# The query projection of a two-block fp32 kernel as three products of rounded parts, and its gate turned later

## The chip, the cores and the metric

The kernel runs on one core of a Trainium2 chip, as one program. The metric is the time of one execution on the device in microseconds (us), lower is better.

## The reference, cut to what matters

Two transformer blocks follow each other, all in fp32. The change lies in the first layer of the second block: its grouped-query attention, over 256 latent tokens and 256 context tokens together (512), with width 1024.

```python
h_lat = x * (1.0 + sc_a) + sh_a
h_ctx = xc * (1.0 + csc_a) + csh_a
...
q, k, v = jnp.split(h @ w_qkv, [16 * 64, (16 + 4) * 64], axis=-1)
q = rms_norm_2(q.reshape(b, n, 16, 64), q_norm)
k = rms_norm_2(k.reshape(b, n, 4, 64), k_norm)
v = v.reshape(b, n, 4, 64)
if rotate:
    q = apply_grid_rope(q, rope)
    k = apply_grid_rope(k, rope)
...
y_lat = block_attention(q_lat, k_all, v_all) @ w_o
y_ctx = block_attention(q_ctx, k_ctx, v_ctx) @ w_o
x = layer_norm(alpha * x + g_a * y_lat, ln_g[i, 0], ln_b[i, 0])
xc = layer_norm(alpha * xc + cg_a * y_ctx, ln_g[i, 0], ln_b[i, 0])
```

Here `x` is what the first block gives, normed by `norm_final`. The context `xc` is an input. The gates `g_a` and `cg_a` are rows of width 1024, one for each stream.

## The kernel before, in words

Every engine has its own program, written out by hand, and semaphores tie them together. A generator per block and engine gives the order; nothing is scheduled by a planner.

- **PSUM.** Eight banks in four pairs: `PROJ`, `SC`, `PT`, `OT`. A `Banks` object knows in which order the fills of a pair follow. `claim` waits until the bank's fill before was taken, `arrived` waits for a fill, `taken` for its release.
- **Weights.** The queue of SyncE (SP) loads tiles of 128 x 4096 numbers (2 MB) into a ring of four slots: `0kv` (keys and values), `0q0`, `0q1` (queries), `0wo0`, `0wo1` (output projection), then the MLP's.
- **Two kinds of matmul.** A plain fp32 `mm` (L2129) leaves two records in the trace. The large ones of the MLPs are done as `product`: each operand is split into a rounded part (`high`, type fp32r) and the rest (`low`), and three fp32r matmuls (L282, L283, L284) replace one plain one. `Split` keeps the weights' parts: GpSimd (POOL) makes `high` by a cast in `round_high` (L263), VectorE (DVE) subtracts and writes `low` over the weight in its slot in `make_low` (L270).
- **The projection, `gqa_project`.** The tokens stand transposed and modulated in `hT` (8 chunks of 128 x 512). PE makes half of the values (`0v1`), and between its two token tiles the transposes of the latent tokens (`xT0`, `xT1`), then ten tiles of 128 rows x 512 tokens, `0a0` to `0a9`: two of keys, eight of queries. Each is eight plain `mm` of 128 x 512. After tile n PE makes the mean square of tile n-1 (`square_mean`) and the rotated halves of tile n-2 (`swap`). ScalarE (ACT) copies and squares tile n, and makes the inverse root for tile n-1 (Ln, then Exp, `scale_of`, L2450 and L2452). DVE multiplies by it (L2671) and rotates (`rotate`, L2659 to L2662). The other half of the values (`0v0`) comes last, and attention waits for the last tiles.
- **The keys' copies.** After each rotated key tile POOL copies it to where attention reads it (L2865, four copies each).
- **The first block's end.** `x_done(t)` is true once DVE has added the last product to token tile t (L1740). ACT then squares the tile (L2557), DVE takes a reciprocal (L2786) and scales the tile by it and by `norm_final` (L2787, a SCALAR_TENSOR_TENSOR whose two wide inputs lie in SBUF). PE's transposes of the latent tiles wait for that.
- **The gate.** `widen` (DVE, L2601) copies a gate's column to all columns, `turn_gate` makes eight transposes on PE (two fills), `take_gate` copies the two fills into `gate_rows` on ACT. For `ga` both streams are turned in the projection, one before `0a0` and one after it.
- **The rest.** Attention over 16 heads, then the output projection (`0wo..`) with residual and layer norm, then the MLP, then the second layer.

In these words T(n) stands for the moment at which ACT begins to copy tile `0a(n)`, which is just after its last matmul.

Of the kernel before, what the change touches and what calls it, by code (L numbers as in the profile page):

```python
# [15 lines left out]
P = 128  # L16
# [44 lines left out]
WORK = 30336  # L61
# [169 lines left out]
class Split:  # L231
# [22 lines left out]
    def high(self, i):  # L254
        _, k, n = self.part(i, True).shape
        return self.buffers[i % len(self.buffers)][:, 0:k * n].rearrange("p (k n) -> p k n", k=k)

    def round_high(self, nc, pool, i):

        self.weights.arrived(pool, self.parts[i][0])  # L260
        if i >= len(self.buffers):
            pool.wait_ge(*self.freed[i - len(self.buffers)])
# [10 lines left out]
    def arrived(self, pe, name, which):  # L273

        i = self.order[name, which]
        pe.wait_ge(self.cut, i + 1)
        return self.high(i), self.part(i, True)

# [41 lines left out]
def first_layer(nc, l, T, dram, out, sem, chip, prev):  # L320
# [204 lines left out]
    for kind, i in step_tiles:  # L525
# [30 lines left out]
    Y = Split(sem, "in", W, chip["ring_low"], chip["ring_high"], parts, freed)  # L556
    halves = [(f"up{i}", b, "n", 2 * P * b, 2 * P) for i in range(8) for b in range(2)]
    halves += [(f"down{i}", b, "k", 2 * b, 2) for i in range(8) for b in range(2)]
    X = Split(sem, "ff", W, chip["ring_low"], early_high + late_high, halves,
              [done(f"up{n}") for n in range(16)] + [(down_used, n + 1) for n in range(15)])  # L560
# [1307 lines left out]
def second_block(nc, T, dram, out, sem, chip, prev):  # L1868
# [8 lines left out]
    hT = work.take(KD, 2 * S)  # L1877
    gate_rows = work.take(2, D)
# [16 lines left out]
    g_v = g.take(4, KV_HEADS * HD)  # L1895
    g_turn = g.take(4, 6, S)
    g_yT = g.take(KD, 2 * S)
    before = Carver(g_turn.rearrange("p a b c -> p (a b c)"))
    g_sq, g_rs, g_rot = before.take(2, 512), before.take(2, 512), before.take(S)
# [56 lines left out]
    for i in range(DEPTH):  # L1956
# [14 lines left out]
        outs += [name for s in range(streams) for name in gate_fills(i, "ga", s)]  # L1971
        outs += [f"{i}o{c}" for c in range(PAIRS)] + [f"{i}wo{t}{h}" for t in range(NT[i]) for h in range(2)]
        score += [name for s in range(streams) for name in gate_fills(i, "gm", s)]
# [16 lines left out]
    GATE = {"ga": OT, "gm": SC}  # L1990
# [62 lines left out]
    X = Split(sem, "mlp", W, chip["ring_low"], half_high, halves, freed)  # L2053
# [7 lines left out]
    nf_scale = sem("nf_scale")  # L2061
    x_first = sem("x_first")
# [25 lines left out]
    cut_base = [0, NT[0] + 2]  # L2088
# [21 lines left out]
    def sync(sp):  # L2110
# [8 lines left out]
        for n, name in enumerate(("ln_g_2", "ln_b_2")):  # L2119
            sp.dma_start(ln_rows[:, n, :], dram[name][0, 0].partition_broadcast(P)).then_inc(first_in, 16)  # L2120
# [6 lines left out]
    def tensor(pe):  # L2127
# [24 lines left out]
        def turn_gate(i, kind, s):  # L2152

            pe.wait_ge(gate_wide, gate_count[i, kind, s])
            for h, name in enumerate(gate_fills(i, kind, s)):
                ps = GATE[kind].claim(pe, name)
# [856 lines left out]
```

## Time and profile before

| what | value |
|---|---|
| median of 3 runs | 2234.24 us (2232.54 to 2234.58) |
| the profiled execution, its own time | 2231.0 us |
| its span, first to last instruction | 2229.2 us |
| mean granted TensorE clock | 0.993 |
| TensorE (PE) busy | 2171.3 us, 97% |
| VectorE, ScalarE, GpSimd busy | 1255.8, 668.7, 484.5 us |

A page of the profile gives busy times by engine. The chain that ended last follows the work back from the last instruction, at each step to what released it. The timeline gives instructions in order of time. Times in all of them count from the start of the span.

### The profile page before, as it was taken

To read this page: it belongs to the slowest core of one execution; us is meant where nothing else is said; L and a number is where in the kernel's file an instruction comes from. 1 tells how busy PE (TensorE), PEld (TensorE's weight loads), DVE (VectorE), ACT (ScalarE), POOL (GpSimd) and SP (SyncE) were. 2 spreads that over 40 slices of the span, in tenths; PEclk is the share of its full clock that TensorE was granted. 3 is DMA by queue.
4 is the path that set the end of the run, shared out by engine and by line. 5 is a ranking of instruction groups with operands and counts; after the bars stand their busy time and mean duration, and the time that the engine had idled before them with its cause. 6 is when DMAs were issued, how large, how long until landed. Compare 5 with 4: busy or idle time off the path is not lost.

```text
span 2229.2 us, 32724 instructions
## 1 busy us (share of the span) xinstructions
PE 2171.3 (97%) x13766; PEld 1768.3 (79%) x13766; DVE 1255.8 (56%) x1678; ACT 668.7 (30%) x1488; POOL 484.5 (22%) x259
## 2 busy tenths in 40 slices
PE   7999999999999999999999999999999999999998
PEld 7998878899889997878898745557888886556887
DVE  5686445865455765449654316665434444457666
ACT  2223453033012234440330267713112023362111
POOL 2222112334322221113433000102111110102332
PEclk9999999999999999999999999999999999999999
DMA  9534667646566346675556503022232314213551
GB/s 267 179 130 141 238 225 225 250 152 227 171 161 224 119 147 225 230 245 200 216 189 218 175 0 120 1 76 95 78 111 78 111 52 106 80 64 123 198 189 57
DMA packets 225959, 339.57 MB, mean 152 GB/s; under 512 B 58988, under 2 KB 94807, under 8 KB 225815
## 3 DMA queue, kind: packets, MB, share of 16 engines
q1 hardware_dynamic: 224720, 333.98, 43.5%
q0 software_dynamic: 944, 3.47, 0.5%
q8 instruction: 110, 1.80, 0.3%
q14 instruction: 35, 0.28, 0.0%
q10 hardware_dynamic: 150, 0.04, 0.0%
HBM read 335.38 MB, written 2.10 MB: 151 GB/s over the span
## 4 chain that ended last, share of the span: by engine, by line
PE 92%; DVE 4%; ACT 2%; issue 1%; SPq 1%; DMA 0%; POOL 0%; DVEq 0%; ACTq 0%
PE bank L282 22%; PE bank L284 21%; PE bank L283 21%; PE bank L2129 15%; PE bank L655 6%; PE bank L2132 2%; PE bank L1000 2%; PE bank L658 1%; SPq L222 1%; DVE ring_low L270 1%; ACT work L1135 1%; ACT L1135 1%; PE bank L952 1%; DVE work L1704 0%; DVE work L1700 0%
## 5 line engine op out<-in xcount | busy, mean ns | idle before, releaser
L283 PE MATMUL bank<-hT_high,ring_low 128*128 128x256 f32 (+1 forms) x2048 | 604.0, 295 | 0.0
L283 PEld LDWEIGHTS bank<-hT_high,ring_low 128*128 128x128 f32 x2048 | 388.8, 190 | 12.2 <-issue 0.7
L263 POOL CAST ring_high<-ring 128x2048 fp32r<-128x2048 f32 (+1 forms) x108 | 204.7, 1895 | 674.8 <-PE bank L284 544.1
L270 DVE TENSOR_TENSOR ring_low<-ring,ring_high 128x2048 fp32r<-128x2048 f32 (+1 forms) x108 | 242.3, 2245 | 123.4 <-POOL ring_high L263 123.2
L282 PE MATMUL bank<-hT_low,ring_high 128*128 128x256 f32 (+1 forms) x1008 | 295.4, 293 | 6.5 <-DVE ring_low L270 4.7
L284 PE MATMUL bank<-hT_high,ring_high 128*128 128x256 f32 (+1 forms) x1008 | 285.0, 283 | 0.0
L263 POOL CAST half_high<-ring 128x2048 fp32r<-128x2048 f32 x64 | 130.5, 2042 | 625.1 <-PE bank L284 452.6
L282 PE MATMUL bank<-ring_low,hidden_high 128*128 128x512 f32 x640 | 251.3, 393 | 0.0
L1135 ACT ACTIVATE work<-bank 128x384 f32<-128x384 f32 (+11 forms) x246 | 109.6, 468 | 386.9 <-PE bank L284 358.3
L270 DVE TENSOR_TENSOR ring_low<-ring,half_high 128x2048 fp32r<-128x2048 f32 x64 | 152.7, 2391 | 95.9 <-POOL half_high L263 95.5
L282 PEld LDWEIGHTS bank<-hT_low,ring_high 128*128 128x128 f32 (+1 forms) x1008 | 192.2, 191 | 15.4 <-issue 8.0
L284 PEld LDWEIGHTS bank<-hT_high,ring_high 128*128 128x128 f32 (+1 forms) x1008 | 190.6, 189 | 0.4
L282 PE MATMUL bank<-hT_low,half_high 128*128 128x256 f32 (+1 forms) x528 | 176.4, 334 | 3.2 <-DVE hT_low L2606 2.5
L284 PE MATMUL bank<-hT_high,half_high 128*128 128x256 f32 (+1 forms) x528 | 176.3, 334 | 0.0
L284 PE MATMUL bank<-half_high,hidden_high 128*128 128x512 f32 x384 | 152.4, 397 | 0.0
L283 PE MATMUL bank<-half_high,hidden_low 128*128 128x512 f32 x384 | 149.8, 390 | 0.0
L2581 ACT ACTIVATE work<-bank 128x512 f32<-128x512 f32 x48 | 28.8, 600 | 375.6 <-PE bank L284 375.6
L282 PEld LDWEIGHTS bank<-ring_low,hidden_high 128*128 128x128 f32 x640 | 119.9, 187 | 26.0
L2129 PE MATMUL bank<-work,ring 128*128 128x512 f32 (+2 forms) x360 | 127.2, 523 | 0.8 <-DVE work L2702 0.6
L2834 DVE TENSOR_TENSOR hidden_low<-work,hidden_high 128x512 fp32r<-128x512 f32 x48 | 37.2, 776 | 148.8 <-ACT work L2584 148.7
L1135 ACT ACTIVATE work<-bank,work 128x256 f32<-128x256 f32 (+2 forms) x168 | 74.0, 449 | 155.7 <-PE bank L284 109.4
L2429 ACT ACTIVATE work<-bank 128x512 f32<-128x512 f32 (+2 forms) x148 | 81.3, 588 | 111.2 <-PE bank L2129 93.6
(242 smaller groups left out, 4441.2 us busy)
## 6 DMA issues: line engine op xcount, KB each, us to landing
ring<-w_ff SPq DMA_DIRECT2D x32, 2048.0 KB, 8.0
ring<-mlp_w SPq DMA_DIRECT2D x32, 2048.0 KB, 8.0
ring<-w_in SPq DMA_DIRECT2D x30, 2048.0 KB, 8.6
ring<-w_ada SPq DMA_DIRECT2D x20, 2048.0 KB, 7.9
ring<-w_branch SPq DMA_DIRECT2D x24, 512.0 KB, 6.5
ring<-w_in SPq DMA_DIRECT2D x32, 256.0 KB, 4.3
ring<-w_out SPq DMA_DIRECT2D x4, 2048.0 KB, 8.4
work<-w_ada SPq DMA_DIRECT2D x4, 2048.0 KB, 13.3
```

The lines of the kernel that those rows point to most:

```text
L263: nc.gpsimd.tensor_copy(self.high(i), self.part(i, False)).then_inc(self.high_made, 1)
L270: nc.vector.tensor_tensor(self.part(i, True), self.part(i, False), self.high(i).bitcast(F32), ALU.subtract)\
L282: nc.tensor.matmul(out, a[0], b[1], start=start, stop=False)
L283: nc.tensor.matmul(out, a[1], b[0], start=False, stop=False)
L284: return nc.tensor.matmul(out, a[0], b[0], start=False, stop=stop)
L655: return nc.tensor.matmul(out, lhsT, rhs, start=start, stop=stop)
L1000: last = nc.tensor.matmul(ps[rows_of, :], silu_c[:, k, at:at + THIN], w[:, k, :], start=n == 0 and k < 4, stop=n == MOD_TILES - 1 and k >= ...
L1135: return nc.scalar.activation(out, in_, func, **kw)
L2129: return nc.tensor.matmul(o, lhsT, rhs, start=start, stop=stop)
L2132: return nc.tensor.transpose(o, src, ident)
L2429: return f(o, src, ACT.Copy, **kw)
L2834: vec.tensor_tensor(hidden_low[:, part, 0:n_tok], hidden[:, part, 0:n_tok], hidden_high[:, part, 0:n_tok].bitcast(F32), ALU.subtract).then ...
```

## The change

1. The eight query tiles are made by `product`. The tokens are split once more: ACT rounds `hT` into `q_hT_high` in four pieces, DVE makes `q_hT_low` in four pieces. The query weights are split in four parts of 256 columns (two tiles each). POOL makes `high` into two buffers `q_high`, which lie where `gate_rows` and `ln_rows` lie, and DVE makes `low`. Parts 0 and 1 are rounded as soon as `x_done` holds for both token tiles; part 2 follows the copies of the first key tile and the end of tile `0a3`, part 3 those of the second and the end of `0a5`.
2. The two gates `ga` are widened, turned and taken behind attention, before the output projection, in banks of `SC` and `PT`, the second one from its own buffer `g_gate`.
3. The rows `ln_g` and `ln_b` are loaded by POOL's queue once all ten tiles are rotated, not by SP's before the fourth weight tile.
4. `in_turn` hands `Split` a list of buffers instead of a rotation; for the other two users the buffers and waits come out the same.

```diff
@@ def second_block: buffers
+    q_high = [chip["rounded"](f"q_high{n}", work.at + n * SPLIT_HALF, SPLIT_HALF) for n in range(2)]
...
+    q_hT_low = chip["rounded"]("q_hT_low", before.at, KD, 2 * S)
...
+    q_hT_high = chip["rounded"]("q_hT_high", g.at, KD, 2 * S)
...
+    g_gate = g_k.rearrange("p a b -> p (a b)").rearrange("p (k j) -> p k j", k=KD)
...
+    q_parts = [(f"0q{j}", b, "n", 256 * b, 256) for j in range(2) for b in range(2)]
+    Q_PARTS = len(q_parts)
+    X_high, X_freed = in_turn(half_high, halves, freed)
+    X = Split(sem, "mlp", W, chip["ring_low"], [q_high[n % 2] for n in range(Q_PARTS)] + X_high, q_parts + halves,
+              [None, None, done(PROJ, "0a3"), done(PROJ, "0a5")] + X_freed)
@@ def sync
-        for n, name in enumerate(("ln_g_2", "ln_b_2")):
-            sp.dma_start(ln_rows[:, n, :], dram[name][0, 0].partition_broadcast(P)).then_inc(first_in, 16)
@@ def tensor: gqa_project
-            turn_gate(0, "ga", 0)
-            pe.wait_ge(first_in, 3 * 16)
+            pe.wait_ge(first_in, 16)
             rows_taken(0, XT_ORDER[0][TT:])
             for n in range(NORMED):
-                if n >= 2 and n % 4 == 2:
-                    w = W.arrived(pe, f"0q{n // 4}")
-                c = n if n < 2 else (n - 2) % 4
-                gemm_T(PROJ.claim(pe, f"0a{n}")[:, :], w, slice(c * P, c * P + P)).then_inc(PROJ.full, 1)
-                if n == 0:
-                    turn_gate(0, "ga", 1)
+                ps, cols = PROJ.claim(pe, f"0a{n}"), slice(n % 2 * P, n % 2 * P + P)
+                if n < 2:
+                    last = gemm_T(ps[:, :], w_kv, cols)
+                else:
+                    if n % 2 == 0:
+                        w = X.arrived(pe, *q_parts[n // 2 - 1][0:2])
+                    if n == 2:
+                        pe.wait_ge(hT_cut, Q_CUTS)
+                    for k in range(KD):
+                        last = product(nc, ps[:, :], [part[:, k, cols] for part in w],
+                                       [part[:, k, :] for part in (q_hT_high, q_hT_low)], k == 0, k == KD - 1)
+                last.then_inc(PROJ.full, 1)
...
             attention(i)
+            if i == 0:
+                for s in range(2):
+                    turn_gate(0, "ga", s)
@@ def scalar: gqa_project
+            for t in XT_ORDER[0]:
+                row_banks(0, t).taken(act, *[f"0xT{t}{h}" for h in range(2)])
+            for k in range(0, KD, KD // Q_CUTS):
+                part = slice(k, k + KD // Q_CUTS)
+                copy(q_hT_high[:, part, :], hT[:, part, :]).then_inc(tokens_rounded, 1)
             take_v(1)
-            take_gate(0, "ga", 0)
@@ def vector: gqa_project
-            dve.wait_ge(first_in, 3 * 16)
+            X.make_low(nc, dve, 0)
+            for k in range(0, KD, KD // Q_CUTS):
+                dve.wait_ge(tokens_rounded, k // (KD // Q_CUTS) + 1)
+                part = slice(k, k + KD // Q_CUTS)
+                vec.tensor_tensor(q_hT_low[:, part, :], hT[:, part, :], q_hT_high[:, part, :].bitcast(F32), ALU.subtract)\
+                    .then_inc(hT_cut, 1)
+            X.make_low(nc, dve, 1)
+            dve.wait_ge(first_in, 16)
             for n in range(NORMED + 1):
+                if n in (2, 4):
+                    X.make_low(nc, dve, n // 2 + 1)
...
@@ def gpsimd
+        for t in range(TT):
+            prev.x_done(pool, t)
+        for n in range(2):
+            X.round_high(nc, pool, n)
+        pool.wait_ge(X.high_made, 2)
         for n in range(2):
             pool.wait_ge(roped, n + 1)
...
+            pool.wait_ge(k_copied, 4 * n + 4)
+            X.round_high(nc, pool, 2 + n)
+            pool.wait_ge(X.high_made, 3 + n)
         pool.wait_ge(roped, NORMED)
         pool.dma_start(grid, dram["grid_mla"]).then_inc(grid_in, 16)
+        for n, name in enumerate(("ln_g_2", "ln_b_2")):
+            pool.dma_start(ln_rows[:, n, :], dram[name][0, 0].partition_broadcast(P)).then_inc(ln_in, 16)
```

On POOL, at the start of the second block, the program before had nothing between the last cast of the first block's MLP and the keys' copies. Now these rows stand there:

```order
+L263 CAST q_high_90<-ring 128x2048
+L263 CAST q_high_91<-ring 128x2048
+L2921 COPY work<-work 64x512 x4
+L263 CAST q_high_90<-ring 128x2048
+L2921 COPY work<-work 64x512 x4
+L263 CAST q_high_91<-ring 128x2048
+L2927 DMA work<-grid_mla 128x640
+L2929 DMA work<-ln_g 128x1024
+L2929 DMA work<-ln_b 128x1024
```

The first two casts came ahead of the copies, one more behind each group of four copies, and two DMAs came behind the grid's.

On DVE, from the scaling of the two token tiles (L2786, L2787 before; L2836, L2837 now) on, before:

```order
L2786 RECIPROCAL cos<-cos 128x1
L2787 SCALAR_TENSOR_TENSOR x_sb<-x_sb,cos,work 128x1024
L2619 TENSOR_SCALAR work<-bank,mod 128x128 x8
L2601 COPY work<-mod 128x1024 x2
L2671 SCALAR_TENSOR_TENSOR work<-work,cols 128x512 x2
L2659 TENSOR_TENSOR work<-bank,work 128x256
```

and now:

```order
+L2836 RECIPROCAL cos<-cos 128x1
+L2837 SCALAR_TENSOR_TENSOR x_sb<-x_sb,cos,work 128x1024
+L2661 TENSOR_SCALAR work<-bank,mod 128x128 x8
+L270 TENSOR_TENSOR ring_low_52<-ring,q_high_90 128x8x256
+L2710 TENSOR_TENSOR q_hT_low<-work,q_hT_high 128x1024 x4
+L270 TENSOR_TENSOR ring_low_52<-ring,q_high_91 128x8x256
+L2721 SCALAR_TENSOR_TENSOR work<-work,cols 128x512 x2
+L2700 TENSOR_TENSOR work<-bank,work 128x256
+L2701 TENSOR_TENSOR work<-work 128x256
+L2703 TENSOR_TENSOR work<-work 128x256
+L270 TENSOR_TENSOR ring_low_51<-ring,q_high_90 128x8x256
+L2721 SCALAR_TENSOR_TENSOR work<-work,cols 128x512
```

The gate's two copies went away here, and six subtractions came in before the first key tile is scaled, then one before tile 2 is scaled (and one more, not shown, before tile 4).

On PE, from the first half of the values on (`work` is both the tokens and the gate's buffer), before:

```order
L2132 MATMUL bank<-consts,x_sb 128x128 x16
L2129 MATMUL bank<-ring,work 128x256 x8
L2132 MATMUL bank<-consts,work 128x128 x8
L2129 MATMUL bank<-work,ring 128x512 x8
L2132 MATMUL bank<-consts,work 128x128 x8
L2129 MATMUL bank<-work,ring 128x512 x8
L2129 MATMUL bank<-work,consts 128x512
L2129 MATMUL bank<-work,ring 128x512 x8
```

and now:

```order
L2158 MATMUL bank<-consts,x_sb 128x128 x16
L2155 MATMUL bank<-ring,work 128x256 x8
L2155 MATMUL bank<-work,ring 128x512 x16
L2155 MATMUL bank<-work,consts 128x512
L287 MATMUL bank<-q_hT_low,q_high_90 128x512
L288 MATMUL bank<-q_hT_high,ring_low_52 128x512
L289 MATMUL bank<-q_hT_high,q_high_90 128x512
```

Both groups of eight gate transposes left this place, the two key tiles stand together, and from the third tile on three matmuls stand for each plain one.

## Rows read from the trace of the kernel before

**Rows 1.** The profile page: the chain that ended last, by engine.
```profile
PE 92%; DVE 4%; ACT 2%; issue 1%; SPq 1%; DMA 0%; POOL 0%; DVEq 0%; ACTq 0%
```

**Rows 2.** The chain in 1240 to 1500 us: start, duration, what, how many.
```profile
1267.90 0.87 PE bank L2132 x8
1268.77 6.87 PE bank L2129 x16
...
1439.17 0.73 issue
```

**Rows 3.** Timeline of the handover: start, duration, engine, line, operation, count.
```profile
1259.24 0.69 DVE L1740 TENSOR_TENSOR x_sb<-x_sb,bank 128x512 f32<-128x512 f32 x1
...
1260.04 1.28 DVE L2787 SCALAR_TENSOR_TENSOR x_sb<-x_sb,cos,work 128x1024 f32<-128x1024 f32 x1
...
1262.01 1.28 DVE L2787 SCALAR_TENSOR_TENSOR x_sb<-x_sb,cos,work 128x1024 f32<-128x1024 f32 x1
1262.50 1.95 PE L2132 MATMUL bank<-consts,x_sb 128*128 128x128 f32 x16
...
1264.28 3.62 PE L2129 MATMUL bank<-ring,work 128*128 128x256 f32 x16
```

**Rows 4.** Timeline of one query tile, the last one.
```profile
1340.09 0.60 ACT L2429 ACTIVATE work<-bank 128x512 f32<-128x512 f32 x1 [3.13 <-PE bank L2129]
...
1341.18 7.03 PE L2129 MATMUL bank<-work,ring 128*128 128x512 f32 x16
...
1345.15 0.75 DVE L2671 SCALAR_TENSOR_TENSOR work<-work,cols 128x512 f32<-128x512 f32 x1 [6.28 <-ACT work L2452]
...
1348.24 0.60 ACT L2429 ACTIVATE work<-bank 128x512 f32<-128x512 f32 x1 [3.13 <-PE bank L2129]
```

**Rows 5.** Timeline where the first key tile is rotated and POOL copies it.
```profile
1297.66 0.42 DVE L2662 TENSOR_TENSOR work<-work 128x256 f32<-128x256 f32 x1
...
1298.15 2.62 POOL L2865 COPY work<-work 64x512 f32<-64x512 f32 x4 [60.65 <-DVE work L2662]
```

**Rows 6.** Timeline in the MLP: first and last of ten products' matmuls in a row.
```profile
1600.00 0.40 PE L284 MATMUL bank<-hT_high,half_high 128*128 128x512 f32 x1
...
1602.09 0.40 PE L284 MATMUL bank<-hT_high,half_high 128*128 128x512 f32 x1
```

**Rows 7.** Timelines where a cast and a DVE operation begin together, and L1532's durations (min/median/max).
```profile
762.87 1.90 POOL L263 CAST ring_high<-ring 128x2048 fp32r<-128x2048 f32 x1 [5.68 <-PE bank L284]
762.91 2.39 DVE L1532 TENSOR_TENSOR work<-work 128x512 f32<-128x512 f32 x1
...
L1532 DVE TENSOR_TENSOR work<-work x16: 678/1444/2390, 107.4 to 788.4; 128x512 f32<-128x512 f32 x16
...
253.89 2.06 DVE L1650 TENSOR_SCALAR work<-work 128x256 f32<-128x256 f32 x1
...
253.91 1.90 POOL L263 CAST ring_high<-ring 128x2048 fp32r<-128x2048 f32 x1 [12.93 <-DMA ring<-w_in]
```

**Rows 8.** Timeline where casts and subtractions take turns in layer one's start.
```profile
1439.25 3.73 POOL L263 CAST half_high<-ring 128x2048 fp32r<-128x2048 f32 x2 [77.83 <-PE bank L2129]
1441.17 3.95 DVE L270 TENSOR_TENSOR ring_low<-ring,half_high 128x2048 fp32r<-128x2048 f32 x1 [10.71 <-POOL half_high L263]
...
1442.92 3.95 POOL L263 CAST half_high<-ring 128x2048 fp32r<-128x2048 f32 x1
```

**Rows 9.** Groups of instructions by shape: the splitting's operations (busy us, mean ns).
```profile
L1135 ACT ACTIVATE y_high<-work 128x1024 fp32r<-128x1024 f32 x1 | 1.1, 1062 | 0.0
...
L2606 DVE TENSOR_TENSOR hT_low<-work,hT_high 128x1024 fp32r<-128x1024 f32 x4 | 4.9, 1226 | 0.1
```

**Rows 10.** Durations of L270 with the MLP's buffers (min/median/max).
```profile
L270 DVE TENSOR_TENSOR ring_low<-ring,half_high x64: 2277/2286/3973, 1441.2 to 2206.4; 128x2048 fp32r<-128x2048 f32 x64
```

**Rows 11.** Windows: PE busy, the other engines, then granted clock (PEclk).
```profile
1348.20:1363.00 14.80, 12.45 (x53) 8.61 (x53) 7.40 (x17) 11.38 (x17) 0.68 (x1) 0.99 0.29 98
...
1500.00:1700.00 200.00, 198.09 (x904) 162.15 (x903) 95.67 (x92) 40.58 (x70) 34.63 (x19) 1.00 0.28 99
```

More of the change, by code:

```diff
@@ L277, in arrived, with in_turn @@
         return self.high(i), self.part(i, True)
+def in_turn(buffers, parts, used):
+    return [buffers[i % len(buffers)] for i in range(len(parts))], [None] * len(buffers) + used
 def product(nc, out, a, b, start, stop):
@@ L1970, in second_block @@
         turned += [f"{i}t{h + e}_{u}" for h, u in units for e in range(2)]
-        outs += [name for s in range(streams) for name in gate_fills(i, "ga", s)]
+        if i == 1:
+            outs += gate_fills(1, "ga", 0)
         outs += [f"{i}o{c}" for c in range(PAIRS)] + [f"{i}wo{t}{h}" for t in range(NT[i]) for h in range(2)]
+        if i == 0:
+            score += gate_fills(0, "ga", 0)
+            turned += gate_fills(0, "ga", 1)
         score += [name for s in range(streams) for name in gate_fills(i, "gm", s)]
@@ L1989, in second_block, with gate_bank, gate_source @@
     SCORE = (SC, PROJ)
-    GATE = {"ga": OT, "gm": SC}
+    def gate_bank(i, kind, s):
+        return SC if kind == "gm" else ((SC, PT)[s] if i == 0 else OT)
+    def gate_source(i, kind, s):
+        return g_gate if (i, kind, s) == (0, "ga", 1) else gate_src
     def row_banks(i, t):
@@ L2154, in turn_gate @@
             pe.wait_ge(gate_wide, gate_count[i, kind, s])
+            bank, src = gate_bank(i, kind, s), gate_source(i, kind, s)
             for h, name in enumerate(gate_fills(i, kind, s)):
-                ps = GATE[kind].claim(pe, name)
+                ps = bank.claim(pe, name)
                 for k in range(4):
-                    last = turn(ps[:, k * P:k * P + P], gate_src[:, 4 * h + k, :])
-                last.then_inc(GATE[kind].full, 1)
+                    last = turn(ps[:, k * P:k * P + P], src[:, 4 * h + k, :])
+                last.then_inc(bank.full, 1)
         def gemm_T(o, w, cols, n=2 * S, chunks=KD, src=None):
@@ L2568, in scalar @@
             attention(i)
+            if i == 0:
+                for s in range(2):
+                    take_gate(0, "ga", s)
             for t in range(NT[i] + 1):
@@ L2795, in vector @@
                 modulate(i, f"{i}xT{t}1", t, 0, banks=row_banks(i, t))
-            if i == 0:
-                widen(0, "ga", 0)
-                widen(0, "ga", 1)
             (gqa_project, mla_project)[i]()
             attention(i)
+            if i == 0:
+                for s in range(2):
+                    widen(0, "ga", s)
             own = len(halves) // DEPTH
@@ L2806, in make @@
                 if n < own:
-                    X.make_low(nc, dve, own * i + n)
+                    X.make_low(nc, dve, Q_PARTS + own * i + n)
             for n in range(3):
                 make(n)
-            OT.taken(dve, *gate_fills(i, "ga", NT[i] // TT - 1))
+            for s in range(NT[i] // TT):
+                gate_bank(i, "ga", s).taken(dve, *gate_fills(i, "ga", s))
             for t in range(NT[i] + 1):
@@ L2881, in highs @@
             for n in range(first, stop):
-                X.round_high(nc, pool, own * i + n)
+                X.round_high(nc, pool, Q_PARTS + own * i + n)
         highs(0, 0, 3)
```

49 lines of the change are left out of this document (27 added, 22 removed).

## The prediction

> **What bounds the kernel now.** I read the page first. TensorE is busy for 97% of the span, and the chain that ended last runs through it for 92% [rows 1]. So an edit counts by what it does to TensorE's own sequence, and by the few waits in it. Next I read the chain around the second block's projection. It goes straight through PE: eight gate transposes take 0.87 us, then the first key tile's eight matmuls 6.87 us [rows 2]. Of the query tiles none waits: from T(8) at 1340.09 to T(9) at 1348.24 are 8.15 us [rows 4], and that is 6.87 for the tile, 0.86 for `square_mean` (two of the tile's sixteen records, 6.87/16 = 0.43 each) and 0.43 for `swap` (half as wide). In those 8.15 us ACT, DVE and POOL are done long before the next tile comes: DVE has scaled tile 8's predecessor at 1345.15 + 0.75 = 1345.90, 5.8 us behind T(8) [rows 4]. The other place to see is the handover between the blocks, in the timeline. `x_done` for the second tile comes at 1259.24 + 0.69 = 1259.93; DVE scales the tiles from 1260.04 and 1262.01, 1.28 us each, until 1263.29; PE's sixteen transposes start at 1262.50, so the second eight start at about 1263.5, and PE has hardly a tenth of slack there: the next matmuls start at 1264.28 [rows 3].
>
> **The change, part by part.**
>
> *The tiles.* The MLP has the same product with the same shape (128x128 weights, 512 columns, fp32r). From the first to the last of ten matmuls in a row, 1600.00 to 1602.09, nine gaps are 2.09 us, 0.232 each [rows 6]. A tile of 24 takes 5.57 us against 6.87, so eight tiles give back 8 x 1.30 = **10.4 us**. The period of a query tile falls from 8.15 to 6.86.
>
> *The gates leave the projection.* Two groups of eight transposes at 0.87 [rows 2] give back **1.74 us**. Their DVE copies and ACT copies lay beside the matmuls, so they give nothing.
>
> *The gates at the output projection.* There the chain has 0.73 us of waiting, PE being held until ACT has copied the last head pair [rows 2]. The sixteen transposes start in that gap: 1.74 - 0.73 = **1.0 us** is lost. The widening stands on DVE behind its last scaling of probabilities, some matmuls of PE before the gap. ACT takes the gates while PE makes the first output tile of 6.87 us. Without either cover each of these would cost some 2 us.
>
> *Rounding the tokens.* ACT's four pieces take 1.06 each by the nearest row, an fp32r cast of 128x1024, together 4.2 us; DVE's four take 1.23, together 4.9 [rows 9]. Both start when the last token tile is modulated and have the two key tiles, 13.7 us of PE, as cover. They end about 7 us before tile 2 starts, two subtractions of 2.28 [rows 10] among them. ACT's release of `0v1` is later by 4.2 us, but it is wanted only when tile 1 starts. I take nothing; uncovered it would be 9 us.
>
> *Parts 2 and 3 of the weights.* The first key tile is rotated 1297.66 + 0.42 = 1298.08, and POOL starts 0.07 later and copies for 2.62 [rows 5]. T(2) is six periods of 8.15 before T(8), 1291.2, so POOL is free at T(2) + 9.6. With the new period that is T(3) + 2.8. Cast (1.90 [rows 7]) and subtraction (2.28) follow, and end at T(3) + 7.1. The part itself is wanted by tile 6, at T(5) + 1.1, 7.7 us later. But behind the subtraction on DVE stands the scaling of tile 2 (0.75), and PE's `swap` of that tile waits for it. It is ready at T(3) + 7.9. PE starts the next tile 1.09 behind T (1341.18 against 1340.09 [rows 4]), and the `swap` 0.43 before that, so it comes to it at T(4) + 0.66 = T(3) + 7.5. That is a wait of **0.4 us**; before it had 2 us to spare. For part 3 tile 5's end comes later than the copies: cast and subtraction end at T(5) + 4.3, before the root for tile 4 is there at T(5) + 5. No wait.
>
> *The two first casts.* This is the part that costs most, and nothing in the diff shows it. POOL starts casting part 0 when `x_done` holds. That is the moment at which DVE starts to scale the two latent tiles, on the path of PE. The trace shows what happens when a cast and a DVE operation meet. At 762.87 a cast starts and 0.04 us later a DVE operation with two inputs in SBUF, which takes 0.68 alone; it takes 2.39, and ends 0.53 behind the cast. At 253.91 a cast starts 0.02 us after a DVE operation and still holds it, for 2.06 [rows 7]. Where both have more to do they alternate: a cast from 1439.25, a second behind it, the subtraction from 1441.17 held for 3.95 instead of 2.28, the third cast held for 3.95 in its turn, until 1446.87, which is 1.75 behind the end of that subtraction [rows 8, 10]. So it is whole operations that exclude each other. L2787 has two wide inputs in SBUF.
>
> By [rows 5] POOL starts 0.07 us after the DVE operation that frees it: 1259.93 + 0.07 = 1260.00, DVE's L2787 at 1260.04. The cast comes first, by about the margin of 762.87. Then: cast until 1261.90; the first scaling is over 1.28 - 0.15 = 1.13 behind it, at 1263.03 (0.15 is what 0.68 lost in the row); the second cast until 1264.78; the second scaling until 1265.91, against 1263.29. PE starts the second eight transposes at about 1266.0 instead of 1263.5. That is **2.45 us** on PE; the 3.46 us of the values' second half still hide the modulation behind it. The bounds: nothing, if such an operation isn't held, and 3.7, if each scaling lies behind a whole cast without overlap.
>
> The Trainium skill, "SBUF — State Buffer", section "Who interferes with whom", says the same of the kinds: a DVE instruction with two SBUF inputs contends with a GpSimd instruction that reads SBUF, and whoever issues first has the ports for the whole instruction. By this rule alone a cast at 1260.05 instead of 1260.00 would be the second, and the loss 0.75 instead of 2.45; the trace agrees on the exclusion, but its 253.91 shows that a cast can win from 0.02 behind.
>
> *The rows of the norm and the two DMAs on POOL.* They are wanted in the MLP, behind attention and output projection, and POOL has nothing else to do in attention. SP's weight tiles come about 1 us earlier and wait for their slots as before. Nothing.
>
> *The end of the projection.* From T(9) on the same operations follow in the same order, so attention moves as T(9) does.
>
> Sum: -10.4 - 1.74 + 1.0 + 0.4 + 2.45 = **-8.3 us**. The profiled execution took 2231.0 us and would take 2222.7. The three timed runs have their median 3.2 us higher, at 2234.24, so the forecast is 2226.0 there.
>
> **The rivals.**
>
> *The scaling wins the first meeting.* If POOL needs a tenth more for its five waits, the first cast waits for the first scaling (until 1261.32), ends at about 1263.1, and the second scaling, due at 1262.01, ends at 1264.2 instead of 1263.29. PE loses 0.75. For it: the margin is 0.04 us. Against it: 253.91. The sum is -10.0: 2224.3.
>
> *No meeting costs anything.* If this operation is not held, or the casts come late (weights not landed), the sum is -10.7: 2223.5. Against it speak [rows 7, 8].
>
> *The tiles are held by the others.* The new period leaves 1.9 us behind the 5 that ACT needs for a tile, where 3.1 were. If the root, the scaling or a late part makes PE wait in most of the eight periods, 0.5 us in each, 4 us more go: -4.3, 2230. For it: one such wait is already in my sum. Against it: only the tiles with a subtraction in front of them are tight.
>
> *The granted clock falls.* The one way to a slower kernel that I see. PE would wait 2.45 us where it did not wait, and the second half of the projection has a denser pattern. At the lower level, 1.2 GHz, a tile of 5.57 would take 11.1. All eight would cost 44.6, and 19% of that stretch, 8.3 us, uses up the gain; half of it gives +14: 2248. Against it: with 2.35 us of waiting in 14.8 the granted clock was 0.99, and 200 us of this product were at 1.00 [rows 11].
>
> **How the numbers follow.** My forecast has 0.60, the scaling first 0.18, no cost 0.09, the tiles held 0.09, the clock 0.04. The predicted time is that of the first, 2226.0. The range goes down to the third rival's 2223.5 and a microsecond below, since the three runs differ by 2 us, and up to the fourth's 2230 and a little more: 2222.5 to 2230.8. A measurement of this kernel tells some 0.2%, 4.5 us, from no change. The first three cases are faster by more, as good as all their chance, 0.87; the tiles held is on the edge, and counts as the same, 0.09; the clock is slower, 0.04.
>
> **What would show it.** Query tiles of 24 matmuls in about 5.57 us and periods of 6.86. The operation L2837 (L2787 before) twice, held to about 3.0 and 2.8 us, with casts of q_high around it, and PE's second eight transposes about 2.5 us later than the first. One wait of about 0.4 us for L2721 before the `swap` of tile 2. The first two gate fills directly behind the last head pair. T(9) about 9.3 us earlier than 1348.24, and the output projection about 8.3 earlier than 1439.9. Wrong would be: scalings of 1.28 us, waits for L2721 in every period, a query tile of over 6 us, or a granted clock below 1 in the projection.

## The result, and the profile after

| kernel | median us | runs | ratio to before, 95% interval |
|---|---|---|---|
| before, runs beside the first measurement | 2233.39 | 4 | |
| after, first measurement | 2220.99 (2218.79 to 2223.45) | 4 | 0.9949 [0.9934, 0.9964] |
| after again, second chip | 2222.57 | 5 | 0.9963 [0.9950, 0.9975] |
| after again, third chip | 2223.03 | 5 | 0.9963 [0.9950, 0.9977] |

The change makes the kernel faster, by 0.4 to 0.5%. The first measurement gives -12.4 us, the two repeats -8.7 (against 2231.23, 17 runs of before) and -7.6 (against 2230.65, 9 runs). The forecast was -8.3 us, and 2226.0 in absolute terms, with 2222.5 as the low end; the first median lies 1.5 us below that end.

Two parts of the profile page of after, its busy times and the chain by engine. The profiled execution took 2223.45 us.

```profile
PE 2164.6 (97%) x13830; PEld 1781.9 (80%) x13830; DVE 1271.0 (57%) x1686; ACT 672.2 (30%) x1492; POOL 493.4 (22%) x265
...
PE 91%; DVE 4%; ACT 3%; issue 1%; POOL 0%; DMA 0%; ACTq 0%; DVEq 0%; POOLq 0%
```

PE is the bound as before [rows 1]. DVE and POOL have the splitting on top, and their share of the chain has not grown.

The handover of after, in the timeline, answers to [rows 3] (L2837 is the old L2787, L1747 the old L1740):

```profile
1258.62 1.38 DVE L1747 TENSOR_TENSOR x_sb<-x_sb,bank 128x512 f32<-128x512 f32 x2 [1.37 <-PE bank L289]
...
1260.11 1.29 DVE L2837 SCALAR_TENSOR_TENSOR x_sb<-x_sb,cos,work 128x1024 f32<-128x1024 f32 x1
1260.25 5.74 POOL L263 CAST q_high<-ring 128x2048 fp32r<-128x2048 f32 x2 [22.68 <-DVE x_sb L1747]
...
1262.08 2.15 DVE L2837 SCALAR_TENSOR_TENSOR x_sb<-x_sb,cos,work 128x1024 f32<-128x1024 f32 x1
...
1264.29 1.09 PE L2158 MATMUL bank<-consts,x_sb 128*128 128x128 f32 x8 [0.68 <-DVE x_sb L2837]
1265.21 3.62 PE L2155 MATMUL bank<-ring,work 128*128 128x256 f32 x16
```

`x_done` holds at 1258.62 + 1.38 = 1260.00. DVE's first scaling starts 0.11 later and takes its usual 1.29. POOL's cast starts 0.25 later, behind it. Only the second scaling is held, 2.15 instead of 1.28. PE's next matmuls start 5.10 us behind the first scaling; before it was 1264.28 - 1260.04 = 4.24. The loss is 0.86.

The query tiles in the timeline of after answer to [rows 4, 6]:

```profile
1296.58 0.59 PE L2155 MATMUL bank<-work 128*128 128x256 f32 x2
...
1296.82 0.58 PE L287 MATMUL bank<-q_hT_low,q_high 128*128 128x512 f32 x1
...
1300.74 2.29 DVE L270 TENSOR_TENSOR ring_low<-ring,q_high 128x2048 fp32r<-128x2048 f32 x1 [4.75 <-POOL q_high L263]
...
1302.35 0.40 PE L289 MATMUL bank<-q_hT_high,q_high 128*128 128x512 f32 x1
1302.59 1.02 PE L2155 MATMUL bank<-work,consts 128*128 128x512 f32 x2
1302.79 0.60 ACT L2464 ACTIVATE work<-bank 128x512 f32<-128x512 f32 x1 [1.84 <-PE bank L289]
1302.95 0.75 DVE L2721 SCALAR_TENSOR_TENSOR work<-work,cols 128x512 f32<-128x512 f32 x1
...
1303.76 0.70 PE L2155 MATMUL bank<-work 128*128 128x256 f32 x2
...
1310.07 0.60 ACT L2464 ACTIVATE work<-bank 128x512 f32<-128x512 f32 x1 [2.24 <-PE bank L289]
```

The lines from 1296.82 to 1302.35 are the first and the last matmul of tile `0a4`. T(4) is 1302.79 and T(5) 1310.07, 7.28 apart. The other intervals from T(2) to T(9) are 6.86 or 6.87, as forecast. The 0.4 too much is the wait before tile 2's `swap`: the scaling L2721 starts at 1302.95 only, behind the subtraction L270, and the `swap` at 1303.76, 0.97 behind T(4). The `swap` before it started at 1296.58, 0.66 behind T(3), which is 1295.92.

The chain of after where the heads end (start, duration, what) answers to the last two lines of [rows 2]:

```profile
1426.39 3.75 PE bank L2155 x32
1430.13 1.90 PE bank L2158 x16
1432.03 20.60 PE bank L2155 x48
```

The chain gives the gates 1.90 there, and the gap of 0.73 is gone. That would be 1.17 lost, but the chain counts each group from the end of the one before it, and the records of matmuls overlap. So the loss is better read between two starts: from the first matmul of the last head pair (1435.36 before, 1426.32 now) to the 13th matmul record of the output projection (1445.13 and 1437.02) PE needed 9.77 us and needs 10.70. The gates cost 0.93.

**Where the time lies.** The span of each profiled execution is cut at three moments: the first scaling (L2787 or L2837), T(9), and the 13th matmul record of the output projection (below "the 13th matmul" for short). Each column is a difference of two starts in that execution's trace. The projection's first matmul would be a worse landmark. Behind a wait it is 0.50 to the next start instead of 0.43, and behind the gates' transposes its record starts 0.16 ahead of their end. From the second on all starts lie 0.43 apart in every run.

| execution | to first scaling | from there to T(9) | from there to the 13th matmul of the output projection | from there to the end | span |
|---|---|---|---|---|---|
| before | 1260.04 | 88.20 | 96.89 | 784.07 | 2229.2 |
| before, another | 1257.85 | 88.20 | 96.90 | 784.06 | 2227.0 |
| after | 1260.11 | 77.43 | 99.49 | 784.64 | 2221.7 |
| after, second | 1259.84 | 77.45 | 98.23 | 784.06 | 2219.6 |
| after, third | 1261.44 | 77.41 | 98.31 | 784.08 | 2221.2 |
| casts late | 1260.17 | 76.59 | 98.35 | 784.04 | 2219.1 |
| casts early | 1259.58 | 79.16 | 97.03 | 786.07 | 2221.8 |
| gates only | 1262.03 | 87.14 | 98.34 | 784.07 | 2231.6 |
| gates and rows | 1258.71 | 86.45 | 98.33 | 784.10 | 2227.6 |
| plain tiles | 1260.51 | 87.31 | 98.49 | 783.99 | 2230.3 |
| gates in attention | 1260.72 | 77.43 | 96.48 | 785.13 | 2219.8 |
| gates in attention, second | 1263.06 | 77.42 | 96.48 | 783.96 | 2220.9 |
| three edits | 1258.13 | 76.15 | 96.48 | 785.28 | 2216.0 |
| three edits, second | 1261.15 | 76.14 | 96.49 | 785.44 | 2219.2 |

The column to T(9) repeats within 0.04 us for one kernel. The one before it, which no edit touches, differs by up to 5.2 us. So steps of half a microsecond are read from the column to T(9), and never from the times.

### The profile page after: what moved, and what is told of

The parts are those of the page before. It is cut to its first block, busy times and chain, and to the rows that moved or that the text cites. A ratio compares the mean times of both kernels' runs of the same rounds, so it can differ in the third digit from the quotient of the medians.

```text
span 2221.7 us, 32882 instructions
## 1 busy us (share of the span) xinstructions
PE 2164.6 (97%) x13830; PEld 1781.9 (80%) x13830; DVE 1271.0 (57%) x1686; ACT 672.2 (30%) x1492; POOL 493.4 (22%) x265
## 4 chain that ended last, share of the span: by engine, by line
PE 91%; DVE 4%; ACT 3%; issue 1%; POOL 0%; DMA 0%; ACTq 0%; DVEq 0%; POOLq 0%
PE bank L287 23%; PE bank L289 22%; PE bank L288 22%; PE bank L2155 12%; PE bank L662 6%; PE bank L2158 2%; PE bank L1007 2%; PE bank L665 1%; DVE ring_low L270 1%; ACT work L1142 1%; ACT L1142 1%; PE bank L959 1%; DVE work L1711 0%; DVE work L1707 0%; DMA work<-nsa_cmp_pos_v 0%
## 5 line engine op out<-in xcount | busy, mean ns | idle before, releaser
L270 DVE TENSOR_TENSOR ring_low<-ring,ring_high 128x2048 fp32r<-128x2048 f32 (+1 forms) x108 | 242.2, 2245 | 120.7 <-POOL ring_high L263 120.6
L270 DVE TENSOR_TENSOR ring_low<-ring,half_high 128x2048 fp32r<-128x2048 f32 x64 | 152.6, 2390 | 94.7 <-POOL half_high L263 94.3
L2155 PE MATMUL bank<-work 128*64 128x256 f32 (+5 forms) x538 | 110.6, 461 | 4.3 <-ACT work L2565 3.7
L2155 PE MATMUL bank<-ring,work 128*128 128x512 f32 (+1 forms) x288 | 112.0, 545 | 0.5 <-issue 0.5
```

What stands on the lines that cost most here:

```text
L270: nc.vector.tensor_tensor(self.part(i, True), self.part(i, False), self.high(i).bitcast(F32), ALU.subtract)\
L2155: return nc.tensor.matmul(o, lhsT, rhs, start=start, stop=stop)
```

## The experiments

### The changed kernel again, and where its casts start

The kernel of after once more, as a base.

> The changed kernel once more, nothing edited, to tell its size from the spread of few runs. Theory A (the trace's terms hold: eight tiles at 1.30, gates 1.74 out and 1.16 in with the gap, the second scaling held for 0.9, PE held 0.4 before a swap, and the rest of the measured gain is the spread by the length of the half-clock stretch at attention's start): -9 to -11 us against the kernel before, and a profile whose T(9) lies 10.7 us before that of the kernel before, as in the first one, while its end may differ by 2 to 4 us with the length of that stretch. Theory B (a term is mis-sized, some 2 to 4 us more are gained after T(9)): -12 to -13 us, and the end of the projection to the end of the span shorter than before by that.

Its median is 2222.57, -8.7 against before and so a little less than the expected -9 to -11. T(9) is 77.45 behind the first scaling, and the way to the end isn't shorter than before's: the trace of after repeats, and the expected theory B is out.

**Casts late.** They wait until the latent tiles are scaled.

```diff
-        for t in range(TT):
-            prev.x_done(pool, t)
+        pool.wait_ge(x_first, TT)
```

> The first two casts of q_high wait until both scalings of the latent tiles are done (x_first) instead of x_done. Theory A: both scalings take 1.28 us, PE's second eight transposes follow the first without the 0.68 us wait, T(9) comes 0.9 us earlier than in the changed kernel, and nothing else waits, because the subtractions have some 7 us to spare. Rival: the casts collide with DVE's token subtractions instead (1266 to 1274) and tile 2 starts late; then T(9) is later, not earlier.

**Casts early.** POOL waits for the weights first, and of `x_done` for its last semaphore alone (`x_last`, which is the wait for the last of the four products' releases). The first cast's own wait for the weights is left out.

```diff
-        for t in range(TT):
-            prev.x_done(pool, t)
+        W.arrived(pool, "0q0")
+        prev.x_last(pool)
```

> POOL waits for the weights first and then for the one semaphore that comes last, so that the first cast starts some 0.2 to 0.3 us earlier, at about the moment of the first scaling. This asks for the price that the forecast took, the cast winning the first meeting: the scalings held to about 3.0 and 2.8 us, PE's second transposes 2.45 us behind those of the kernel before, T(9) 1.6 us later than in the changed kernel, +1.6 us in the time. Rival (the scaling wins even at equal starts): first scaling 1.29, second 2.0 to 2.2, no change of the time against the changed kernel.

Timeline of casts late:

```profile
1260.17 1.29 DVE L2837 SCALAR_TENSOR_TENSOR x_sb<-x_sb,cos,work 128x1024 f32<-128x1024 f32 x1
...
1262.14 1.28 DVE L2837 SCALAR_TENSOR_TENSOR x_sb<-x_sb,cos,work 128x1024 f32<-128x1024 f32 x1
...
1263.49 3.74 POOL L263 CAST q_high<-ring 128x2048 fp32r<-128x2048 f32 x2 [25.86 <-DVE x_sb L2837]
...
1264.41 3.62 PE L2155 MATMUL bank<-ring,work 128*128 128x256 f32 x16
...
1266.27 3.10 DVE L270 TENSOR_TENSOR ring_low<-ring,q_high 128x2048 fp32r<-128x2048 f32 x1
```

Timeline of casts early (its lines are up to four higher):

```profile
1258.09 1.38 DVE L1748 TENSOR_TENSOR x_sb<-x_sb,bank 128x512 f32<-128x512 f32 x2 [1.37 <-PE bank L290]
...
1259.58 2.99 DVE L2841 SCALAR_TENSOR_TENSOR x_sb<-x_sb,cos,work 128x1024 f32<-128x1024 f32 x1
1259.60 4.72 POOL L264 CAST q_high<-ring 128x2048 fp32r<-128x2048 f32 x2 [22.57 <-DVE x_sb L1748]
...
1262.68 2.72 DVE L2841 SCALAR_TENSOR_TENSOR x_sb<-x_sb,cos,work 128x1024 f32<-128x1024 f32 x1
...
1266.39 2.97 PE L2159 MATMUL bank<-ring,work 128*128 128x256 f32 x13
```

Late: both scalings take 1.28 or 1.29, PE's matmuls follow 4.24 behind the first as before, and T(9) comes 0.86 earlier than in the run beside it (76.59 against 77.45). The collision now falls on the subtraction (3.10 instead of 2.28), where the key tiles cover it. Early: the cast starts 0.02 behind the scaling and still has the ports. The scalings take 2.99 and 2.72, where the forecast had 3.0 and 2.8, and the matmuls follow 6.81 behind the first, a loss of 2.57 where the forecast had 2.45. T(9) comes 1.71 later than beside it. So the forecast's price for a cast that comes first was right, and what was wrong here was which comes first. The times (2221.41 and 2223.64 against 2222.57) point the same way, but even the difference between the ends, 2.2 us, is within the spread of the runs.

### The gates without the tiles, and with the norm's rows

Both kernels are before, with the two gates turned behind attention as in after. In gates and rows the rows of the norm are on POOL's queue as well; this is its diff against gates only, shortened.

```diff
-        for n, name in enumerate(("ln_g_2", "ln_b_2")):
-            sp.dma_start(ln_rows[:, n, :], ...).then_inc(first_in, 16)
...
-            pe.wait_ge(first_in, 3 * 16)
+            pe.wait_ge(first_in, 16)
...
+            pool.dma_start(ln_rows[:, n, :], ...).then_inc(ln_in, 16)
```

> The kernel before with only the two ga gates moved behind attention, their own banks and buffer included; tiles plain, norm rows loaded by SP as before. Forecast's terms: T(9) 1.74 us earlier, 1.0 us given back at the output projection, so -0.7 us, within 0.2%. After the changed kernel's trace, in which the sixteen transposes took 1.90 on the chain: -0.6. Theory B would allow -2 to -4 here, if moving the gates is what shortens the rest.

> The kernel before with the gates behind attention, as in gate_only, and the norm rows loaded by POOL's queue behind the last rotation as in the changed kernel. In gate_only PE waited 0.42 us for the DMA of ln_b before the first key tile, and that tile ended 0.68 later than the gate's removal alone would put it. Theory: that wait was hidden by the gate's transposes before, and moving the rows is the part of the change that takes it away: T(9) at 86.5 from the first scaling, against 87.14 in gate_only. Rival: PE waits for the small grid load on the same queue anyway, and T(9) stays at 87.1. The times can't tell 0.7 us.

Gates only: 2231.24, 1.0001 [0.9992, 1.0009]. Gates and rows: 2230.64, 1.0002 [0.9993, 1.0011]. Moving the gates is worth nothing that the time can tell. The trace shows more. Waits of PE in gates only, in the timeline:

```profile
1268.65 1.24 PE L2139 MATMUL bank<-ring,work 128*128 128x256 f32 x5
1270.31 1.13 PE L2139 MATMUL bank<-work,ring 128*128 128x512 f32 x2 [0.42 <-DMA work<-ln_b]
```

PE waits in front of the first key tile until the norm's second row has landed. In before the gate's transposes covered that. T(9) is 87.14 behind the first scaling, only 1.06 less than before, and with the rows moved it is 86.45, 1.75 less. So the rows' move, which the forecast put at nothing, is worth 0.69: without it the gates' removal brings 1.06 and not 1.74.

### The tiles without the products

In after, each query tile is made of eight plain matmuls again. They multiply the tokens by the low parts of the weights alone, so the product itself is left out; all casts, subtractions and waits stay.

```diff
-                        last = product(nc, ps[:, :], [part[:, k, cols] for part in w],
-                                       [part[:, k, :] for part in (q_hT_high, q_hT_low)], k == 0, k == KD - 1)
+                        last = mm(ps[:, :], w[1][:, k, cols].bitcast(F32), hT[:, k, :], k == 0, k == KD - 1)
```

> The changed kernel with its eight query tiles made by plain fp32 matmuls again (16 records a tile), while all casts, roundings and subtractions stay. It multiplies the tokens by the low part of the weights only, so this part of the computation is left out. T(9) is counted here from the start of the first scaling of a latent tile (88.20 us before, 77.43 in the changed kernel, 76.59 with the casts late, 79.16 with them early). Forecast's term: eight tiles at 1.30 us, and the 0.4 us wait before a swap gone, since the period is 8.15 again: T(9) at 87.4, +10 us in the time, and the kernel equal to the one before to 0.1% (+1 to +2 us: the gate's 1.2 and the held scaling's 0.9, less 1.74). Theory B (the gain is not in the tiles): +6 us or less.

The time is 2232.11, 1.0007 [0.9999, 1.0016], against 2218 to 2224 for the kernels with the products: nearly all of the gain is theirs. T(9) is 87.31, 9.88 more than in after. Eight tiles at 1.30 are 10.4, and the wait of 0.4 before the `swap` is gone with the longer period; 10.0 is left.

### The gates in attention's waits

The gates are turned at attention's start, behind the first scores and two steps on, in banks of `OT`. PE's waits for ACT are there.

```diff
             for n in range(units + LAG[i]):
+                if i == 0 and n in (0, 2):
+                    turn_gate(0, "ga", n // 2)
...
-            if i == 0:
-                for s in range(2):
-                    turn_gate(0, "ga", s)
```

> The changed kernel with both ga gates turned at the start of attention, the first behind the first pair of scores, where PE waits 2.0 us for ACT, the second two score pairs later, in the banks of OT. T(9) stays at 77.4 from the first scaling. If those transposes lie in PE's waits: the output projection starts 1.2 us earlier relative to the last head pair (the sixteen transposes took 1.90 on the chain, and the 0.73 us wait for the last copy comes back), and the total is -1 to -1.9 us. Rival: ACT's four copies of 0.6 us in the start of attention, where ACT and DVE set the pace, cost as much as they save: 0 +- 0.5. If idle PE time is what drops the clock, the half-clock stretch at 1352 (7 to 10 us long) should get shorter or vanish, worth up to 3 us more.

The median is 2218.85, and the ratio to before 0.9952 [0.9939, 0.9964]. The way from T(9) to the 13th matmul of the output projection falls to 96.48 from after's 98.2 to 99.5. That is more than the 0.93 of the gates, and the windows show the rest. Each line has a stretch of 2 us, PE's busy time, the weight loads', DVE's, ACT's and POOL's, then the granted clock. First after, then gates in attention, at the same place of the program.

```profile
1350.00:1352.00 2.00, 0.05 (x2) 0.08 (x2) 1.96 (x5) 1.64 (x5) 1.62 (x3) 1.00 1.05 402
1352.00:1354.00 2.00, 1.75 (x10) 1.07 (x12) 1.88 (x6) 1.25 (x4) 0.23 (x1) 0.65 1.05 409
1354.00:1356.00 2.00, 1.74 (x4) 0.17 (x2) 1.93 (x7) 1.71 (x7) 0.00 (x0) 0.50 1.05 420
1356.00:1358.00 2.00, 1.53 (x4) 0.54 (x4) 1.93 (x7) 1.28 (x5) 0.00 (x0) 0.50 0.98 303
1358.00:1360.00 2.00, 2.00 (x9) 1.53 (x8) 1.92 (x6) 0.97 (x3) 0.00 (x0) 0.50 1.02 410
1360.00:1362.00 2.00, 2.00 (x11) 1.22 (x9) 0.99 (x3) 1.74 (x5) 0.00 (x0) 0.50 1.05 408
1362.00:1364.00 2.00, 2.00 (x14) 1.37 (x12) 1.48 (x4) 1.13 (x4) 0.00 (x0) 0.79 1.05 410
```

```profile
1350.00:1352.00 2.00, 1.80 (x11) 0.81 (x9) 1.70 (x4) 1.66 (x5) 1.01 (x2) 1.00 1.04 400
1352.00:1354.00 2.00, 1.09 (x9) 0.79 (x9) 1.93 (x6) 1.68 (x7) 0.71 (x2) 1.00 1.04 404
1354.00:1356.00 2.00, 2.00 (x14) 1.14 (x12) 1.96 (x5) 1.54 (x6) 0.00 (x0) 1.00 1.06 423
```

In after PE had 0.05 us of work in two, and then the clock was at 1.2 GHz (0.50) for 10.2 us. In gates in attention, where PE's wait there is 1.1 us instead of 2.0, it stayed at 2.4 GHz. It was at 1.2 GHz for 3.4 us in before, and for 6.8 in the other two executions of after, casts late, gates only, gates and rows and plain tiles. In casts early it did not fall, though PE waits the same 2.0 us as in after; there the way is 97.03. So PE's pause doesn't decide alone whether the clock falls.

As far as that one execution tells, the way without a fall and without gates takes 97.03 - 0.93 = 96.10. Against that before's stretch of 3.4 costs 0.8 (96.89). Against 97.03 the stretches of 6.8 cost 1.2 to 1.5 (98.23 to 98.49), and the one of 10.2 costs 2.5 (99.49). The gates in attention cost 96.48 - 96.10 = 0.4 themselves. Against an after with 6.8 this version is 1.8 shorter on that way: 0.5 or 0.6 from the gates, the rest from the clock.

What the clock gives here is mostly given back. In one execution of gates in attention and in both of the three edits (below) the clock falls for 3.4 us at about 1494 to 1498, and the way to the end takes 785.1 to 785.4 instead of 784.1. Casts early has such a fall as well, at 1499.5. So four of the five executions without a fall at attention's start have one there, and none of the nine with one. Why they go together is open.

### The three edits together

Casts late, gates in attention, and the subtractions of parts 2 and 3 moved behind the scalings of the next tile:

```diff
-                if n in (2, 4):
-                    X.make_low(nc, dve, n // 2 + 1)
+                if n in (3, 5):
+                    X.make_low(nc, dve, (n + 1) // 2)
```

> The changed kernel with three edits: the first casts wait for both scalings (as in casts_late, T(9) 0.84 earlier), DVE's subtractions for parts 2 and 3 stand one tile later (before tiles 3 and 5 are scaled), which should take away the 0.4 us wait before the third swap, and the gates turned at attention's start as in gates_gap. Sum -0.84 - 0.4 - 1.2: T(9) at 76.2 from the first scaling, -2.4 us against the changed kernel, -11 us against the kernel before. Rival: the subtraction one tile later makes another product or swap wait; then T(9) is at 76.6 or later.

The median is 2218.16, and the ratio to before 0.9951 [0.9938, 0.9965]. T(9) is 76.15 behind the first scaling: 0.86 for the casts and 0.42 for the `swap`, whose wait is gone. In the timeline the scaling of tile 2 now comes before the subtraction:

```profile
1298.13 0.75 DVE L2721 SCALAR_TENSOR_TENSOR work<-work,cols 128x512 f32<-128x512 f32 x1 [4.99 <-ACT work L2483]
...
1299.93 2.28 DVE L270 TENSOR_TENSOR ring_low<-ring,q_high 128x2048 fp32r<-128x2048 f32 x1
1299.94 0.60 ACT L2459 ACTIVATE work<-bank 128x512 f32<-128x512 f32 x1 [1.84 <-PE bank L289]
...
1306.81 0.60 ACT L2459 ACTIVATE work<-bank 128x512 f32<-128x512 f32 x1 [1.84 <-PE bank L289]
```

### All once more, on one chip

Before with a profile, after, gates in attention and the three edits, to compare them beside each other.

> The kernel before, nothing edited, for a second profile. Theory A says that T(9) and the operations repeat to 0.1 us (88.20 from the first scaling) and that what differs between two executions is where and how long the clock is at its half level: 30 us in sum in the first profile, 3.5 of it at attention's start (1362 to 1366). Expected: T(9) at 88.2, the half-clock stretches in sum anywhere from 25 to 37 us.

> The changed kernel a third time, on the chip on which the next two run. Its size so far is -12.4 us by the medians of four runs, -8.7 by the second job. Theory A: -8 to -10 us by the medians, T(9) at 77.4, and a half-clock stretch of 7 to 10 us at attention's start (1352 to 1362), as in both profiles so far. Theory B: -12 or more.

> gates_gap once more, beside the changed kernel on one chip. If the transposes in PE's wait keep the clock up at attention's start: no half-clock stretch in 1345 to 1366 again, and 2 to 4 us less than the changed kernel by the medians (1.2 from the transposes, the rest from the clock, some given back by a stretch near 1497). If the missing stretch was chance: it is there again in this profile, and the gain is 1.2 us or less.

> all_edits once more on that chip. T(9) at 76.15; 1.3 us less than gates_gap_2 by its terms (0.84 for the late casts, 0.4 for the swap), which the times may just show: -10 to -13 us against the kernel before, the fastest of the three.

| kernel | median us, runs | ratio, 95% interval |
|---|---|---|
| before | 2230.65, 9 | |
| before, the profiled execution | 2228.81, 1 | |
| after | 2223.03, 5 | 0.9963 [0.9950, 0.9977] |
| gates in attention | 2222.43, 5 | 0.9963 [0.9950, 0.9975] |
| three edits | 2220.38, 5 | 0.9952 [0.9939, 0.9964] |

In the table of stretches every column to T(9) repeats, and the first one moves by 5.2 us between these four. Before's stretches at 1.2 GHz are 23 us in sum, where 25 to 37 were expected. After is 7.6 us under before, a little less than the expected 8 to 10. Gates in attention has no stretch at attention's start again, and its 1.8 us up to the output projection, but only 0.6 in the medians, where 2 to 4 were expected. The three edits are the fastest version here and in the measurement before, 2.65 below after here. The traces make it 3.1 from the first scaling to the output projection's 13th matmul (172.63 against 175.72), of which 1.2 and 1.4 go again behind it, where the clock falls at about 1497 (785.28 and 785.44 against 784.1). The intervals overlap, so the times alone don't prove its lead over after.

## Why the prediction was right and wrong, step by step

**The tiles, -10.4: right.** The period is 6.86 to 6.87. Without the products the whole gain is gone (2232.11).

**The gates out of the projection, -1.74, and the rows of the norm, nothing: right together, wrong apart.** T(9) gains 1.75 with both and 1.06 with the gates alone. The forecast asked who wants the rows, found the MLP, and missed that PE's own wait stood behind them (`first_in`, 3 * 16, in the diff). The gate that the change removed was that wait's cover.

**The wait before the swap, +0.4: right**, by place, cause and size.

**The failed step: "The cast comes first, by about the margin of 762.87."** This is the term of +2.45, and 0.86 was measured in its place. POOL started 0.25 us behind `x_done`, not the 0.07 of [rows 5]. That 0.07 is the start behind a single wait, and here five stand in a row. The trace shows where the rest goes: between the event at 1260.01 and the cast at 1260.25 POOL has two instructions that do nothing but wait, which end at 1260.08 and 1260.17. In casts early there is one such instruction, and the cast comes 0.13 behind the event; in casts late there is none, and it comes 0.07 behind. The scaling, 0.11 behind `x_done`, was first, and PE lost 0.86 instead of 2.45. The forecast's first rival, "the scaling wins the first meeting", had exactly this case, with 0.75 for it and a chance of 0.18. When the cast is let loose 0.13 behind, it wins and costs 2.57. The price was right and the order wrong, and the order hung on 0.1 us. T(9) came 10.77 us earlier instead of 9.3: 1.6 by this step, less 0.1 of rounding.

The Trainium skill, "SBUF — State Buffer", section "Who interferes with whom", says that whoever issues first has the shared ports for the whole instruction. The traces agree where the cast is 0.14 behind the scaling (1260.25 and 1260.11): the scaling takes its usual 1.29, and the first cast 2.90 instead of 1.90. In casts early the scaling starts 0.02 ahead by the records and is held all the same, as at 253.91 in [rows 7]: so starts 0.02 apart in the records don't tell which of the two has the ports.

**The gates at the output projection, +1.0: right**, measured 0.93.

**"From T(9) on the same operations follow in the same order, so attention moves as T(9) does": wrong by 0.4 to 1.7 us.** From T(9) to the 13th matmul of the output projection after needs 98.2, 98.3 or 99.5 where before needs 96.9. Of that 0.93 are the gates, and the rest is the time at the lower clock at attention's start, 6.8 or 10.2 us instead of 3.4. Gates only has it too, without any product. What in the new order makes the stretch longer is open; that it isn't the same in two executions of one kernel is shown.

**The sum.** From the first scaling to the 13th matmul of the output projection before takes 185.09. After takes 176.91, 175.69 and 175.72: -8.2, -9.4 and -9.4, where the forecast had -8.3. That the first is so near is luck: the cast's 1.6 too much and the clock's 1.7 too little met in it. Behind that point nothing is gained: before takes 784.07 and 784.06, after 784.06 and 784.08 in two executions and 784.64 in the first, where the clock is low for 6.8 us near 2028 and not for 3.4.

**The time itself, 2226.0: wrong by the base.** The forecast took -8.3 off 2234.24, a median of three runs. Before's later runs have their medians at 2231.23 (17), 2231.08 (21) and 2230.65 (9), some 3 us lower, and go from 2227.43 to 2234.61. The forecast's own other base, the profiled 2231.0, gave 2222.7, and the 14 runs of after in the three measurements have their median at 2222.55. The first four of them happened to have two of the three lowest. So the size held, within a microsecond by luck as said, and the range was too narrow on its low side: it had a term for each mechanism and none for the base. Whether the first three runs were slow by their chip or by chance no run tells.

**The other rivals, no cost of any meeting, the tiles held, the clock fallen in the projection:** none of them came. Query tiles ran at the full clock in all executions.

## What to carry to other kernels

When two engines are released by the same event and exclude each other, work out both orders and take the release that makes the order certain: a wait one step later cost nothing here and gave 0.86 us on the path of PE. Before you call a moved load free, look for waits that count it, besides the work that reads it. A base of three runs is itself uncertain, here by 3 us of 2231, more than most of the terms; read small steps between two landmarks of one trace, where they repeat within 0.04 us, and choose landmarks that have the same instructions at the same pace around them in both kernels: the first matmul behind a wait and the first behind other matmuls are not the same mark.

## What the runs showed of the hardware that was not expected

- **Stretches at half clock wander.** In every profiled execution there are five to eight places where the granted clock is at 1.2 GHz, for 3.4 to 10.2 us each, 23 to 36 us in sum. The same kernel has other ones each time: ahead of the first scaling before had 17.1 us of them and then 10.2, and came to it at 1260.04 and 1257.85. At attention's start, set against casts early, 3.4 us of it cost 0.8, 6.8 cost 1.2 to 1.5 and 10.2 cost 2.5. The runs' spread goes with it: before at a mean clock of 0.995 or 0.996 takes 2227.4 to 2229.7, at 0.991 about 2233.5. Other executions with equal sums differ by 2 to 3.5 us at the first scaling, so it isn't the whole of it.
- **Waits that are already met take time where they are instructions of their own.** POOL's start came 0.25 us behind the last event with two such instructions in between, 0.13 with one, and 0.07 with none (casts late, and [rows 5]).
- **A product is three matmuls of 0.232 us with rounded operands where a plain one is 0.859**, in the projection as in the MLP, from where the forecast had it: the period of a query tile fell from 8.15 to 6.86 wherever the products stand.
